# Windowed attention with the two masked key blocks regrouped into a near block and a half-width far block

## What is computed

```
def block(i):
    start = i * Q_BLOCK
    kb = lax.dynamic_slice_in_dim(kp, start, 3 * Q_BLOCK, axis=1)     # key blocks i-1, i, i+1
    ...
    valid = ((jnp.abs(qpos[:, None] - kpos[None, :]) <= WINDOW)
             & (kpos >= 0)[None, :] & (kpos < L)[None, :])
    ...
    p = jax.nn.softmax(jnp.concatenate([s_lat, s_ctx, sink_col], axis=-1), axis=-1).astype(v.dtype)
```

## Time and profile before

| | |
|---|---|
| median of 3 runs | 2286.06 us (2285.43 to 2286.56) |
| the profiled execution | 2285.58 us |
| span of its slowest core | 2282.5 us (cores 2279.7 to 2282.5) |
| granted TensorE clock | 0.993 of full speed, mean; 0.994 on one core |
| busy: TensorE matmul, VectorE, ScalarE, GpSimd | 98%, 63%, 52%, 32% |

### The profile page before, as it was taken

How to read it: one execution, slowest core, us unless ns; L and a number is a source line. 1 busy time by engine, 2 the same in 40 slices (tenths; PEclk the granted TensorE clock), 3 DMA queues, 4 the chain that set the end, 5 groups by cost and what they waited for, 6 DMA issues and landing times.

```text
span 2282.4 us, 64875 instructions; the slowest of 8 cores (2279.7 to 2282.5 us)
## 1 busy us (share of the span) xinstructions
PE 2229.5 (98%) x23312; PEld 1320.8 (58%) x23312; DVE 1446.9 (63%) x3896; ACT 1198.0 (52%) x2325; POOL 733.7 (32%) x852
## 2 busy tenths in 40 slices
PE   6789999999999999999999999999999999999998
PEld 1465565565565556556556556555655655655654
DVE  0456666666666666666666666666666666666664
ACT  1256556555555555555644655555555564565553
POOL 0232333333233233233333323323323323333332
PEclk9899999999999999999999999999999999999999
DMA  9991332332333343333333233334333323323312
GB/s 245 227 178 45 80 77 69 78 81 70 73 89 71 73 80 71 73 80 76 71 78 90 66 77 89 71 70 83 71 73 80 75 71 78 80 68 76 80 45 66
DMA packets 234303, 193.64 MB, mean 85 GB/s; under 512 B 197492, under 2 KB 205812, under 8 KB 231432
## 3 DMA queue, kind: packets, MB, share of 16 engines
q1 hardware_dynamic: 231544, 168.45, 31.3%
q0 software_dynamic: 2448, 21.04, 5.0%
HBM read 125.02 MB, written 33.56 MB: 69 GB/s over the span
## 4 chain that ended last, share of the span: by engine, by line
PE 94%; DMA 2%; DVE 1%; ACT 1%; issue 1%; POOL 0%; SPq 0%; another core or an unknown queue 0%; DVEq 0%; POOLq 0%; ACTq 0%
PE pb L573 31%; PE pb L580 23%; PE pb L812 10%; PE pb L870 10%; PE pb L740 7%; PE pb L766 6%; PE pb L804 5%; DMA s_PT<-x 2%; PE pb L354 1%; DVE s_yb L775 0%; ACT s_PT L743 0%; PE pb L526 0%; POOL s_kT L612 0%; DVE s_hT L532 0%
## 5 line engine op out<-in xcount | busy, mean ns | idle before, releaser
L573 PE MATMUL pb<-s_W,s_hT 128*128 128x512 bf16 (+1 forms) x3584 | 771.5, 364 | 0.0
L743 ACT ACTIVATE s_PT<-pb 128x512 bf16<-128x512 f32 x1264 | 652.5, 605 | 74.4 <-PE pb L740 73.6
L580 PEld LDWEIGHTS pb<-s_hT,s_W 128*128 128x128 bf16 x9216 | 525.2, 98 | 105.3 <-issue 82.7
L580 PE MATMUL pb<-s_hT,s_W 128*128 128x128 bf16 x9216 | 571.8, 220 | 1.4 <-DVE s_hT L532 0.5
L573 PEld LDWEIGHTS pb<-s_W,s_hT 128*128 128x128 bf16 x3584 | 337.9, 98 | 309.6 <-issue 1.7
L793 ACT ACTIVATE s_Tm<-pb 128x512 bf16<-128x512 f32 x256 | 153.1, 598 | 389.4 <-PE pb L573 308.3
L645 DVE TENSOR_TENSOR s_scr<-pb,s_ropet 128x512 f32<-128x512 f32 x256 | 165.0, 686 | 143.4 <-PE pb L580 142.9
L612 POOL TENSOR_TENSOR s_kT<-s_scr 128x128 bf16<-128x128 f32 x128 | 93.6, 731 | 474.7 <-DVE s_scr L609 449.8
L816 POOL TENSOR_TENSOR s_mg<-s_ub,s_scr 128x512 bf16<-128x512 f32 x128 | 161.9, 1265 | 255.3 <-DVE s_scr L797 255.3
L812 PE MATMUL pb<-s_wmf,s_ybT 128*128 128x512 bf16 x1024 | 242.5, 380 | 0.0
L775 DVE SCALAR_TENSOR_TENSOR s_yb<-pb,s_small,s_Gb 128x64 bf16<-128x64 f32 x1024 | 220.1, 277 | 28.3 <-DVE s_small L772 1.3
(11 more groups left out here) (115 smaller groups left out, 2183.1 us busy)
## 6 DMA issues: line engine op xcount, KB each, us to landing
s_xr<-x SPq DMA_DIRECT2D x63, 512.0 KB, 4.9
y<-s_xr SPq DMA_DIRECT2D x63, 512.0 KB, 2.7
s_xt<-x SPq DMA_DIRECT2D x62, 512.0 KB, 4.6
s_W<-w_in POOLq DMA_DIRECT2D x10, 1024.0 KB, 32.0
s_ropet<-rope SPq DMA_DIRECT2D x64, 128.0 KB, 2.0
s_wmf<-w_mod SPq DMA_DIRECT2D x2, 2048.0 KB, 13.5
s_W<-w_mod SPq DMA_DIRECT2D x2, 2048.0 KB, 27.6
s_wmf<-w_mod POOLq DMA_DIRECT2D x2, 2048.0 KB, 17.9
```

The lines of the kernel that those rows point to most:

```text
L573: E("pe", lambda e, k=k: e.matmul(out=pb[:, c0:c0 + n], lhsT=h[:, k, :], rhs=W[:, wblk, k, c0:c0 + n], start=(k == 0), stop=(k == 7)), rea ...
L580: E("pe", lambda e, c=c, k=k: e.matmul(out=pb[:, c * 128:(c + 1) * 128], lhsT=W[:, wblk, k, c * 128:(c + 1) * 128], rhs=h[:, k, :], start= ...
L743: E("act", lambda e, g=g: e.activation(out=PT[:, jb, g, :], in_=banks[g][0][:, :], func=AF.Exp, scale=0.125), reads=[banks[g][1]], writes= ...
```

## The change

The two masked key blocks hold 128 keys each, of which the mask leaves half the pairs. They are cut into halves of 64 keys and regrouped.

- **Near block**: keys 64 to 127 of the previous tile and keys 0 to 63 of the next one, 128 keys, scored against all 128 queries as before (8 matmuls of 128 columns against 512) and masked in place.
- **Far block**: keys 0 to 63 of the previous tile, which only queries 0 to 63 use, and keys 64 to 127 of the next one, which only queries 64 to 127 use. Each half is a matmul of its own with 64 stationary columns against 256 query columns; the first half writes partitions 0 to 63 of a bank and the second partitions 64 to 127. So there are 16 matmuls of 64x256 in place of 8 of 128x512, in the order x, g, half, and four Exp operations of 128x256 in place of 128x512. The results stand in columns 0 to 63 of each head; the mask operations (four of 128x8x64) write the masked value to both halves of the 128 columns, zero where it doesn't belong.
- **Keys**: `kTp` holds the halves in three slots, next tile's first half beside previous tile's second half (`khalf`); `kTo` holds the tile's own keys. GpSimd has four combining operations per tile instead of two, those of `kTp` first.
- **Values**: the ring `Vr` has NV = 3 tiles. `V_edges(p)`, emitted behind `P_kv(p+1)`, makes VectorE copy halves of 64 partitions x 264 elements: two into `VA` (values of the near block) and one into the previous tile's `Vr` (values of the far block).
- **Order and number of blocks**: own, context 0, near, far, context 1, for every tile. Edge tiles have five blocks instead of four. Their near block is also scored in two halves, 16 matmuls of 64x512; halves that don't exist get values of zero, on which `v_ones` sets the ones again when the slot is reused.

```
 def mask_tables():
-    kk = np.arange(128)[:, None]
-    qq = np.arange(128)[None, :]
-    m = np.zeros((128, 2, 128), np.float32)
-    m[:, 0, :] = np.where(qq <= kk, BIG, 0.0)
-    m[:, 1, :] = np.where(kk <= qq, BIG, 0.0)
-    return m.reshape(128, 256)
+    p = np.arange(128)[:, None]
+    q = np.arange(128)[None, :]
+    lo = p < 64
+    m = np.zeros((128, 256), np.float32)
+    m[:, 0:128] = np.where(np.where(lo, p <= q, q <= p), BIG, 0.0)
+    m[:, 128:192] = np.where(lo & (q[:, 0:64] <= p), BIG, 0.0)
+    m[:, 192:256] = np.where(~lo & (p <= q[:, 64:128]), BIG, 0.0)
+    return m
...
-        kT = [sb(f"kT{i}", [128, 2, 128], BF16) for i in range(NR)]
-        Vr = [sb(f"Vr{i}", [128, 4, 66], BF16) for i in range(NR)]
+        kTo = sb("kTo", [128, 2, 128], BF16)
+        kTp = sb("kTp", [128, NV, 2, 128], BF16)
+        Vr = [sb(f"Vr{i}", [128, 4, 66], BF16) for i in range(NV)]
+        VA = sb("VA", [128, 4, 66], BF16)
...
+        zeroed = set()
+
+        def khalf(t, h):
+            sl = (t + 1 - h) % NV
+            return sl * 256 + 64 * h, bf(f"kh{h}_{sl}")
+
+        def V_edges(t):
+            i, o = t % NT, (t - 1) % NV
+            prev, nxt = Vr[o], Vr[(t + 1) % NV]
+            pb_, nb_ = bf(f"Vr{o}"), bf(f"Vr{(t + 1) % NV}")
+
+            def half(dst, h, src, rd, wr):
+                d = pview(dst, 64 * h, 64, 0, [[1, 264]])
+                if src is None:
+                    E("dve", lambda e: e.memset(d, 0.0), writes=[wr])
+                else:
+                    sp_ = pview(src, 64 * h, 64, 0, [[1, 264]])
+                    E("dve", lambda e: e.tensor_copy(out=d, in_=sp_), reads=[rd], writes=[wr])
+
+            half(VA, 1, prev if i > 0 else None, pb_, bf("VA"))
+            half(VA, 0, nxt if i < NT - 1 else None, nb_, bf("VA"))
+            half(prev, 1, nxt if i < NT - 1 else None, nb_, pb_)
+            if i == 0:
+                half(prev, 0, None, None, pb_)
+            if i in (0, NT - 1):
+                zeroed.add(o)
...
+            (o0, b0), (o1, b1) = khalf(t, 0), khalf(t, 1)
+
+            def comb(out, x, dims, wr):
+                E("pool", lambda e: e.tensor_tensor(out=out, in0=view(s, x * 128, dims), in1=view(s, 256 + x * 128, dims),
+                                                    op=(ALU.subtract if x == 0 else ALU.add)), reads=[sb_], writes=wr)
+
             for x in range(2):
-                E("pool", lambda e, x=x: e.tensor_tensor(out=kT[r][:, x, :], in0=s[:, x * 128:(x + 1) * 128], in1=s[:, 256 + x * 128:384 + x * 128],
-                                                         op=(ALU.subtract if x == 0 else ALU.add)), reads=[sb_], writes=[bf(f"kT{r}")])
+                comb(view(kTp, o0 + x * 128, [[o1 - o0, 2], [1, 64]]), x, [[64, 2], [1, 64]], [b0, b1])
+            for x in range(2):
+                comb(kTo[:, x, :], x, [[1, 128]], [bf("kTo")])
...
+        BLOCKS = (("own", 0), ("ctx", 0), ("near", 0), ("far", 0), ("ctx", 1))
 
         def visit(t, jb):
-            kind, idx, mk = blocks_of(t)[jb]
-            b = (t // NT) % 2
+            kind, idx = BLOCKS[jb]
+            i, b = t % NT, (t // NT) % 2
+            prev = t - 1 if i > 0 else t
+            nxt = t + 1 if i < NT - 1 else t
             q = qT[t % 2]
             banks = [next_bank() for g in range(4)]
+
+            def score(g, x, out, lk, rq, kb):
+                E("pe", lambda e: e.matmul(out=out, lhsT=lk, rhs=rq, start=(x == 0), stop=(x == 1)),
+                  reads=kb + [bf(f"qT{t % 2}_{x}")], writes=[banks[g][1]], inc=(x == 1))
+
             for x in range(2):
                 for g in range(4):
-                    if kind == "lat":
-                        lk, kb = pview(kT[idx], 32 * g, 32, x * 128, [[1, 128]]), bf(f"kT{idx}")
+                    pbk = banks[g][0]
+                    edge_tile = kind == "near" and prev + 2 != nxt
+                    if kind == "far" or edge_tile:
+                        n = 512 if edge_tile else 256
+                        for h in range(2):
+                            o, kb = khalf((nxt, prev)[h] if edge_tile else (prev, nxt)[h], h)
+                            rq = [[1, 512]] if edge_tile else [[128, 4], [1, 64]]
+                            score(g, x, pbk[64 * h:64 * h + 64, 0:n], pview(kTp, 32 * g, 32, o + x * 128, [[1, 64]]),
+                                  pview(q, 32 * g, 32, x * 512 + (0 if edge_tile else 64 * h), rq), [kb])
+                        continue
+                    if kind == "own":
+                        lk, kb = pview(kTo, 32 * g, 32, x * 128, [[1, 128]]), [bf("kTo")]
+                    elif kind == "near":
+                        lk, kb = pview(kTp, 32 * g, 32, khalf(nxt, 0)[0] + x * 128, [[1, 128]]), [khalf(nxt, 0)[1], khalf(prev, 1)[1]]
                     else:
-                        lk, kb = pview(kTc[b], 32 * g, 32, x * CTX + idx * 128, [[1, 128]]), bf(f"kTc{b}_{idx}")
-                    rq = pview(q, 32 * g, 32, x * 512, [[1, 512]])
-                    E("pe", lambda e, lk=lk, rq=rq, g=g, x=x: e.matmul(out=banks[g][0][:, :], lhsT=lk, rhs=rq, start=(x == 0), stop=(x == 1)),
-                      reads=[kb, bf(f"qT{t % 2}_{x}")], writes=[banks[g][1]], inc=(x == 1))
+                        lk, kb = pview(kTc[b], 32 * g, 32, x * CTX + idx * 128, [[1, 128]]), [bf(f"kTc{b}_{idx}")]
+                    score(g, x, pbk[:, :], lk, pview(q, 32 * g, 32, x * 512, [[1, 512]]), kb)
+            if kind == "far":
+                for g in range(4):
+                    E("act", lambda e, g=g: e.activation(out=view(PT, (jb * 4 + g) * 512, [[128, 4], [1, 64]]), in_=view(banks[g][0], 0, [[64, 4], [1, 64]]),
+                                                         func=AF.Exp, scale=0.125),
+                      reads=[banks[g][1]], writes=[bf(f"PT{jb}_{g}")] + ([bf(f"st{jb - 2}")] if t == 0 else []))
+                return
             for g in range(4):
                 E("act", lambda e, g=g: e.activation(out=PT[:, jb, g, :], in_=banks[g][0][:, :], func=AF.Exp, scale=0.125),
                   reads=[banks[g][1]], writes=[bf(f"PT{jb}_{g}")] + ([bf(f"st{jb - 2}")] if t == 0 and jb in (2, 3) else []))
 
         def mask(t, jb):
-            mk = blocks_of(t)[jb][2]
...
+            kind = BLOCKS[jb][0]
+            parts = {"near": [(0, 0, 0, 128)], "far": [(64, 0, 192, 64), (0, 0, 128, 64)]}.get(kind, [])
             for hh in range(2):
-                v = view(PT, (jb * 4 + 2 * hh) * 512, [[128, 8], [1, 128]])
+                o = (jb * 4 + 2 * hh) * 512
                 bs = [bf(f"PT{jb}_{2 * hh}"), bf(f"PT{jb}_{2 * hh + 1}")]
-                E("dve", lambda e, v=v: e.tensor_tensor(out=v, in0=v, in1=view(maskb, mk * 128, [[0, 8], [1, 128]]), op=ALU.min),
-                  reads=bs + [bf("maskb")], writes=bs)
+                for co, ci, cm, n in parts:
+                    E("dve", lambda e, co=co, ci=ci, cm=cm, n=n, o=o: e.tensor_tensor(
+                        out=view(PT, o + co, [[128, 8], [1, n]]), in0=view(PT, o + ci, [[128, 8], [1, n]]),
+                        in1=view(maskb, cm, [[0, 8], [1, n]]), op=ALU.min),
+                      reads=bs + [bf("maskb")], writes=bs)
...
-                for jb, (kind, idx, mk) in enumerate(bl):
-                    if kind == "lat":
-                        rv, vb_ = pview(Vr[idx], 0, 128, g * 66, [[1, 65]]), bf(f"Vr{idx}")
+                for jb, (kind, idx) in enumerate(bl):
+                    if kind == "near":
+                        rv, vb_ = pview(VA, 0, 128, g * 66, [[1, 65]]), bf("VA")
+                    elif kind != "ctx":
+                        sl = (t if kind == "own" else t - 1) % NV
+                        rv, vb_ = pview(Vr[sl], 0, 128, g * 66, [[1, 65]]), bf(f"Vr{sl}")
...
             if hasP:
                 P_kv(p + 1)
+            if hasA:
+                V_edges(p)
```

More of the change, by code:

```diff
@@ L229, in build_program @@
         NR = 4
+        NV = 3
         NH = 4
@@ L457, in fold_pool, with v_ones @@
                     E("dve", lambda e, k=k, pb=pb: e.tensor_copy(out=W[:, 1, k, :], in_=pb[:, :]), reads=[pbb], writes=[bf("W1b")])
-        for j in range(NR):
-            E("pool", lambda e, j=j: e.memset(Vr[j][:, :, 64:66], 1.0), writes=[bf(f"Vr{j}")])
+        def v_ones(j):
+            E("pool", lambda e: e.memset(Vr[j][:, :, 64:66], 1.0), writes=[bf(f"Vr{j}")])
+        for j in range(NV):
+            v_ones(j)
         for j in range(BPC):
@@ L603, in P_kv @@
             rp, rpb = ropet, bf("ropet")
-            E("act", lambda e: e.activation(out=Vr[r][:, :, 0:64], in_=view(pb, 256, [[64, 4], [1, 64]]), func=AF.Copy),
-              reads=[pbb], writes=[bf(f"Vr{r}")])
+            if t % NV in zeroed:
+                zeroed.discard(t % NV)
+                v_ones(t % NV)
+            E("act", lambda e: e.activation(out=Vr[t % NV][:, :, 0:64], in_=view(pb, 256, [[64, 4], [1, 64]]), func=AF.Copy),
+              reads=[pbb], writes=[bf(f"Vr{t % NV}")])
             s, sb_ = next_scr()
@@ L746, in mask @@
```

(15 more changed lines are left out.)

## The result

| | before | changed |
|---|---|---|
| median | 2286.36 us (6 runs) | 2379.47 us (6 runs) |
| ratio, 95% interval | | 1.0399 (1.0384 to 1.0415) |
| profiled execution | 2285.58 us, span 2282.5 | 2375.37 us |
| span of the slowest core | 2282.5 us | 2373.8 us |
| busy PE, DVE, ACT, POOL | 98, 63, 52, 32% | 95, 67, 48, 33% |

What follows compares the result with a forecast made beforehand. TensorE's own stream was taken to bound the steady state; far visits -10.2, edge tiles +4.0 and the start -0.5 gave -6.7 us, so 2279.4 us against a median of 2286.06, range 2277 to 2294.

Steps and rivals of the forecast that it cites:

- The far visit: PE's score matmuls of the far block in 60 interior tiles: 0.17 us gained per visit, -10.2 us in all.
- Rivals 1 to 3: In the far visit: loads per row group, 2284.5 us, 0.17; loads serial, 2293, 0.09; column halves not together, 2330, 0.14.
- both loads dear: Lower bound of the far visit's gain on PE, both weight loads per row group slow: 0.11 us per visit.
- The edge tiles and the start: PE's extra visit and value matmuls in four edge tiles, +4.0 us; a wait filled in period 0, -0.5 us.
- the far mask, "costed at nothing": VectorE's four mask operations between query rotation and gate product: 1.70 us, covered by waits, so 0 us of kernel time.
- The price: VectorE's far mask: four operations of 512 elements like L714's 425 ns, 1.70 us.
- The cover: VectorE behind the far mask: gate product some 0.8 us late, against 1.90 us idle ahead of the product at 1041.87.
- this rival: Missing the far mask's cover on VectorE: it has 1.7 us; not made a rival, given no chance.
- The value copies, the key combinations, ScalarE's shorter Exps: Three VectorE copies (0.87 us), two more GpSimd combinations (0.73 us each), ScalarE 0.87 us less per far visit: each 0.

Runs made afterwards that it cites:

- experiment 3: The changed kernel, full computation, with the far mask emitted ahead of P_q instead of behind it: 2277.56 us, ratio 0.9952 to the kernel before.
- experiment 9: The changed kernel, full computation, with GpSimd's two query combinations made to wait until the far mask is done: 2393.55 us, a single run.
- experiment 6: The kernel before with two added minimum operations of 128x8x64 per interior tile at the far mask's place: 2324.22 us, ratio 1.0168.
- experiment 2: The changed kernel with the value copies left out after period 0: 2376.44 us, ratio 1.0359 to the kernel before.
- experiment 4: The kernel before with four added minimum operations of 128x8x64 per interior tile at the far mask's place: 2378.9 us, ratio 1.0365.

## Why the prediction was wrong

- **The far visit: right.** 0.17 us a visit forecast; from the end of the stream ahead (1004.09 and two matmuls of 0.216, 1004.52) to the next projection at 1004.97 it is 0.45 us, 0.46 forecast. The period without the VectorE loss is 33.50 instead of 33.68, 0.18 x 60 = 10.8 us against 10.2. Rivals 1 to 3 were all about this step, and all three fall. One bound was wrong: the 0.11 "both loads dear" doesn't come out of its row, since two loads of 0.061 and 0.015 of starts leave 0.08; nothing hangs on it.
- **The edge tiles and the start: not contradicted.** With the mask out of the way the kernel is 8.6 us faster than before by the medians (experiment 3: 2277.56 against 2286.16), so by difference edges and start cost 10.8 - 8.6 = 2.2 us instead of 3.5. The interval of that ratio reaches from 3 to 19 us of gain, so the two can't be told apart.
- **The failed step: the far mask, "costed at nothing".** Two parts of it. The price: "four operations of 512 elements like L714's 425 ns", 1.70 us. That is what they take without GpSimd beside them (424 in experiment 3, 1.81 us for four in experiment 9). L714 runs at 1021.59, while GpSimd is idle (7.09 us until 1023.46); the mask's place, from 1038.1 on, is where GpSimd works on the query, and the timeline of GpSimd had the row:

```profile
1037.67 2.51 POOL L650 TENSOR_TENSOR s_qT<-s_scr 128x512 bf16<-128x512 f32 x2 [0.49 <-DVE s_scr L645]
1040.13 1.27 POOL L816 TENSOR_TENSOR s_mg<-s_ub,s_scr 128x512 bf16<-128x512 f32 x1
```

Two of the four took 1.18 and 1.31 us. The cover: I let the product be "some 0.8 us late" and put against it the 1.90 us for which the product into `ub` had been idle. That wait didn't belong to the mask alone: between the two stands the merge sum of the second row, which reads `ub`. It ends at 1041.40, 0.47 us before the product at 1041.87, and it moves with the gate product. The order listed such a wait for the other product into `ub` of a period ("waits act,pe,pool"), before and after the change. The real slack at `ub` is 0.22 us. A mask of 2.59 us makes `ub` 0.88 us late (experiment 6), so one of 1.8 us would by estimate have made it late by 0.1 us, within the slack; at 3.46 us it was 1.75 late in most periods (8.58 - 6.83) and 1.93 in the one shown.
- **"The price of the operation would have to double"** was written as the reason to leave this rival out. It did double.
- The value copies, the key combinations, ScalarE's shorter Exps: each costed at nothing, and experiment 2 (for the copies) and the chain of experiment 3, which is PE alone with all of them in it, bear it out.

The kernel before already showed both parts. The eight modulations of one tile by line and duration (min/median/max), and GpSimd's timeline:

```profile
L532 DVE TENSOR_SCALAR s_hT<-s_hT,s_gs,s_sh x8: 303/310/1326, 1048.6 to 1053.3; 128x128 bf16<-128x128 bf16 x8
```
```profile
1048.79 1.26 POOL L816 TENSOR_TENSOR s_mg<-s_ub,s_scr 128x512 bf16<-128x512 f32 x1 [3.88 <-DVE s_scr L797]
```

One of eight like operations takes 1326 ns instead of 310, the one that meets GpSimd's sum. And the end of VectorE's stretch lay close to PE's need of it:

```profile
1018.99 0.98 DVE L532 TENSOR_SCALAR s_hT<-s_hT,s_gs,s_sh 128x128 bf16<-128x128 bf16 x4
```

finishes at 1019.97, while PE's key projection, which reads these four pieces one after another, has started at 1019.58. The matmul that reads the last piece is the eighth:

```profile
1020.11 0.22 PE L580 MATMUL pb<-s_hT,s_W 128*128 128x128 bf16 x1
```

It starts 0.18 us behind the seventh (1019.93), where the others follow at 0.056. So PE waited some 0.12 us for VectorE here, and in 63 of the 66 such groups of 16 of this kernel the step is over 0.12 us. The groups by shape put such waits at 0.5 us in the whole run:

```profile
L580 PE MATMUL pb<-s_hT,s_W 128*128 128x128 bf16 x9216 | 571.6, 220 | 1.2 <-DVE s_hT L532 0.5 <-ACT s_PT L743 0.4 <-issue 0.2
```

That no wait stood in the list was read as slack. In truth there was none at the meeting itself, and 0.22 us ahead of it (experiment 4).

## What to carry to other kernels

A wait that an engine has in the trace is cover for added work only if the work lies behind everything that ends the wait: follow the buffer, not only the engine, and look for the third engine that must read it in between. Price an added VectorE operation by a row that ran beside what will run beside it, GpSimd above all; a group whose maximum is four times its median is a sign to look for such a neighbour. And before an engine's slack is read off its busy share (67% here, and it set the period), look how long ahead of its reader it finishes at the end of the loop.
